# Filler products moved inside two triangular inverses, and a constant 512-column product added at eight places of one of them

## The reference, cut to what matters

```python
def second_block(x, ...):
    for layer in range(DEPTH):
        h = rms_norm_2(x, norm_g[layer])
        cols = split_columns(h @ w_in[layer])
        y_gdn = gdn_branch(cols, ...)      # unit lower triangular solve per chunk
        y_mla = mla_branch(cols, ...)      # softmax(q k^T) v
        y_rwkv = rwkv7_branch(cols, ...)   # a recurrence over the positions
        mix = concatenate([y_gdn, y_mla, y_rwkv]) * silu(cols['gate'])
        x = x + mix @ w_out[layer]
    return rms_norm_2(x, final_norm_g)
```

## Time and profile before

| | us |
|---|---|
| median of 3 runs | 1421.75 |
| lowest and highest | 1419.37 and 1426.42 |
| the profiled execution's own time | 1425.49 |
| its span | 1423.7 |
| TensorE (matmul) busy | 1324.1 (93% of the span) |
| VectorE busy | 745.7 (52%) |
| ScalarE busy | 344.9 (24%) |
| GpSimd busy | 51.5 (4%) |
| mean granted TensorE clock | 0.926 |

### The profile page before, as it was taken

One profiled execution on the slowest core, in us unless ns is written; L12 is line 12 of the kernel. 1 busy time (PEld: TensorE's weight loads), 2 busy tenths in 40 slices (PEclk: granted clock), 3 DMA queues, 4 the chain that ended last, 5 costly groups with the idle time before them and its releaser, 6 DMA issues. The chain is left out here.

```text
span 1423.7 us, 17706 instructions
## 1 busy us (share of the span) xinstructions
PE 1324.1 (93%) x6933; PEld 972.4 (68%) x6933; DVE 745.7 (52%) x1425; ACT 344.9 (24%) x745; POOL 51.5 (4%) x92
## 2 busy tenths in 40 slices
PE   4999989999989999999997998997999898997997
PEld 4877549994447765999443775685885775684783
DVE  0244366675350234677545388557544388557563
ACT  1233311210020242112002221343321221343222
POOL 2000000000000000000000001003000001002000
PEclk9989899999999999999999899998569999999579
DMA  8713106444453330545444331300011431300000
GB/s 254 243 55 118 60 2 219 158 159 176 175 177 118 119 118 1 194 163 177 177 177 162 105 117 60 119 1 1 0 46 57 155 115 59 119 2 1 1 1 30
DMA packets 65978, 149.21 MB, mean 105 GB/s; under 512 B 2225, under 2 KB 8263, under 8 KB 65895
## 3 DMA queue, kind: packets, MB, share of 16 engines
q1 hardware_dynamic: 62608, 141.67, 28.5%
q0 software_dynamic: 1216, 3.52, 1.0%
q10 hardware_dynamic: 2071, 2.87, 0.8%
HBM read 146.96 MB, written 1.07 MB: 104 GB/s over the span
## 5 line engine op out<-in xcount | busy, mean ns | idle before, releaser
L1305 ACT ACTIVATE region<-banks 128x384 f32<-128x384 f32 (+8 forms) x154 | 74.3, 482 | 363.9 <-PE banks L424 138.8
L424 PE MATMUL banks<-hnT,weight_slabs 128*128 128x256 f32 x672 | 154.9, 393 | 4.8 <-DVE hnT L1777 2.8
L424 PEld LDWEIGHTS banks<-hnT,weight_slabs 128*128 128x128 f32 x672 | 132.0, 198 | 27.3 <-issue 4.6
L474 PE MATMUL banks<-weight_slabs,region 128*128 128x512 f32 x256 | 115.1, 592 | 0.0
L1917 DVE TENSOR_TENSOR region<-banks,region 128x128 f32<-128x128 f32 x40 | 11.7, 292 | 152.8 <-PE banks L587 152.2
L474 PEld LDWEIGHTS banks<-weight_slabs,region 128*128 128x128 f32 x256 | 48.5, 190 | 60.3 <-issue 60.3
L474 PE MATMUL banks<-region 128*128 128x512 f32 x192 | 87.6, 592 | 0.0
L1760 DVE TENSOR_TENSOR region<-region 128x256 f32<-128x256 f32 (+23 forms) x160 | 75.5, 472 | 17.5 <-ACT region L1647 12.1
L1760 DVE TENSOR_TENSOR region<-weight_slabs 128x1024 f32<-128x1024 f32 x32 | 39.2, 1225 | 80.6 <-PE banks L474 76.4
L1760 DVE TENSOR_TENSOR region<-weight_slabs,region 128x1024 f32<-128x1024 f32 x64 | 78.2, 1222 | 1.1
L1261 POOL TENSOR_TENSOR region<-region,consts 128x240 f32<-128x240 f32 (+24 forms) x60 | 34.1, 588 | 1034.8 <-DVEq L1769 1000.9
(11 more groups left out here) (351 smaller groups left out, 2153.9 us busy)
## 6 DMA issues: line engine op xcount, KB each, us to landing
weight_slabs<-in_mlp_w SPq DMA_DIRECT2D x32, 2048.0 KB, 8.7
weight_slabs<-in_w_in SPq DMA_DIRECT2D x10, 2048.0 KB, 7.6
weight_slabs<-in_od_w_in SPq DMA_DIRECT2D x6, 2048.0 KB, 7.9
weight_slabs<-in_ev_w_in SPq DMA_DIRECT2D x5, 2048.0 KB, 8.0
weight_slabs<-in_w_out SPq DMA_DIRECT2D x4, 2048.0 KB, 8.1
weight_slabs<-in_ev_w_out SPq DMA_DIRECT2D x2, 2048.0 KB, 8.4
weight_slabs<-in_od_w_out SPq DMA_DIRECT2D x2, 2048.0 KB, 7.7
weight_slabs<-in_w_in SPq DMA_DIRECT2D x2, 2016.0 KB, 7.7
```

What stands on the lines that cost most here:

```text
L424: ins = mm(view(ps, b + i * S, (1, S)), view(slabs, o + k * width + c0, (1, P)), view(hnT, k * S, (1, S)), start=k == 0, stop=k == KC - 1)
L474: ins = mm(view(ps, b, (1, 512)), view(R, act + k * st, (1, P)), view(w, wt + k * step_, (1, 512)), start=n == 0 and k == 0, stop=n == 7 a ...
L1305: say(A(dst, view(ps, b, *(dims or ((1, n),)), np_=np_), ACT.Copy, scale=scale), read("scalar", *key))
```

## The change

In the RWKV inverse, `invert` calls `between("base", -1)` ahead of step 0, where `fill_inverse` now takes three steps of `dense`; the others of the base move to steps 4, 8, 10, 12 and 14 (eight in all as before, so far one at each even step). At the place ("Y", 1) there were two more steps of `dense`, for which nothing was left; two gate products come there now, and the four later places of the gate thus lose the last two of their eight products.

In the delta rule's inverse the gate products of the base steps 8 to 11 move: three to step 14, one to ("Yhalf", 0). A new helper `warm` issues one product of the identity with 512 constant columns into the bank that the ring "five" will hand out next, without taking it; its result is never read, as the next product of that bank starts it anew. It waits for the bank's last reader, as `open_` will. It is called once at eight places: ahead of step 0, after step 14, and at ("Z", 0), ("Y", 1), ("Z", 1), ("VT", 2), ("Z", 2) and ("X", 2). I call it the constant product.

```diff
@@ -402,6 +402,14 @@
             mm = nc.tensor.matmul
+
+            def warm(n, ring="short"):
+
+                b = RINGS[ring][turn[ring] % len(RINGS[ring])]
+                if b in held:
+                    pe.wait_ge(*at(reader.get(held[b], "bank_read_by_vector"), *held[b]))
+                for _ in range(n):
+                    mm(view(ps, b * 512, (1, 512)), IDENT, view(cst, 0, (1, 512)), start=True, stop=True)
@@ -768,6 +776,7 @@
                 H, NS = W.H, W.NS
+                between("base", -1)
                 for k in range(15):
@@ -970,12 +979,12 @@
                 def fill_inverse(what, n):
                     if what == "base":
-                        fill(1 - n % 2)
+                        fill({-1: 3, 4: 1, 8: 1, 10: 1, 12: 1, 14: 1}.get(n, 0))
                         if n == 7:
...
-                    elif (what, n) in (("Y", 0), ("Z", 0), ("Y", 1)):
+                    elif (what, n) in (("Y", 0), ("Z", 0)):
                         fill(2)
@@ -1121,10 +1130,11 @@
-                GATES = {("base", 8): 1, ("base", 9): 1, ("base", 10): 1, ("base", 11): 1, ("Yhalf", 0): 1, ("Zhalf", 0): 1, ("Yhalf", 1): 1, ("Zhalf", 1): 1}
+                GATES = {("base", 14): 3, ("Yhalf", 0): 2, ("Zhalf", 0): 1, ("Yhalf", 1): 1, ("Zhalf", 1): 1}
+                WARM = (("base", -1), ("base", 14), ("Z", 0), ("Y", 1), ("Z", 1), ("VT", 2), ("Z", 2), ("X", 2))
                 def mla_between(what, n):
-                    if what == "base":
+                    if what == "base" and n >= 0:
                         next(up_steps, None)
@@ -1134,6 +1144,8 @@
                         mla_transpose(PROBS[what, n])
+                    if (what, n) in WARM:
+                        warm(1, "five")
                     for _ in range(GATES.get((what, n), 0)):
```

## The result

The changed kernel takes 1373.96 us (median of 4 runs, 1372.09 to 1376.5), the kernel before 1421.89 (4 runs beside them, 1419.37 to 1426.42). The ratio is 0.9661, with a 95% interval of 0.9632 to 0.969: 48 us faster. The forecast was 1375, with a range from 1360 to 1406.

The account below looks back on a forecast made before the run. TensorE, busy almost without a break and often at half clock, was taken to set the length. The six parts sum to -49.7: 1375.8 against the profiled execution, 1372 against the median; forecast 1375, range 1360 to 1406.

Parts of the forecast that it names:

- Parts 1 and 2: RWKV inverse, both layers: moved products fill pauses and restore full clock; -9.7 for its base, -6.8 for its levels.
- The charge of 1.2 us for steps without fill: RWKV inverse's base: time added back because products left without fill wait for GpSimd's rows, 0.76 us each.
- the RWKV fills change nothing: Rival: GpSimd's picks set the RWKV base, so the RWKV gains halve; 1383 us, chance 0.10.
- Part 3: Delta rule inverse's base: four gate products leave steps 8 to 11, and the pause behind step 14 is filled; -5.8.
- Part 4: Level 0 of the delta rule's inverse: clock still falls at the longer pause ahead of Z; 20 us, net 0.
- only pauses matter: Rival: filled pauses alone keep the clock, also in level 0 (15.5 us) and the tail; 1361, chance 0.10.
- Part 5: Delta rule's inverse, level 1 to its end: full clock from dense products grouped ahead of Y; 22.4 us, -15.6.
- Part 6: Behind the inverse to the output products (tail): two thirds of the possible clock gain, -11.8, between 0 and -17.2.
- the clock stays low: Rival: narrow products keep the delta rule's inverse and tail at the low clock; 1415, against the median 1411, chance 0.14.
- slower: Rival: constant products all lengthen the path if the clock falls early and does not return; 1442, chance 0.04.

Follow-up runs that it names:

- without Z of level 0: The changed kernel without the constant product ahead of Z of level 0; 1381.31 us, ratio 0.9682.
- that pause: gates: The changed kernel with two gate products, moved from between the halves of Y and Z, replacing the constant product in level 0's pause; 1365.27 us, ratio 0.9564.
- the last two of the table: The kernel with gate products in level 0's pause, constant products kept only at three places (1379.27 us), or at all but the base's two (1375.33 us).

## Why the prediction was right

The cause it named holds: TensorE sets the length of these stretches, and the gain is the clock. Point by point:

- *Parts 1 and 2* (-9.7 and -6.8 forecast, -9.0 and -6.7 measured) hold: the RWKV edit alone won 15.7 us in its own stretches. The fall is gone in all 22 layers that have the edit. The edit filled the pause and regrouped the steps behind it at once, so that the pause alone was the cause, as I had taken it, fits but is not isolated. The charge of 1.2 us for steps without fill was the right kind: the row at 885.13 waits 0.83 us, though for VectorE's subtraction and not for GpSimd's picks, as the forecast had it. The rival "the RWKV fills change nothing" falls.
- *Part 3* (-5.8, measured -4.5; its own terms, -3.44 and +0.45 per layer, give -6.0) took the clock of the base as given. The base has a pause of its own, 2.84 us ahead of L1084, in which VectorE does six instructions of the attention (L2519 to L2525, 968.65 to 971.38) between two steps, and the clock fell behind it in both layers (0.93 for the base). Layer 3 had been free of that, so it won only 1.4. What stands behind B 14 put Y off by 0.37 us, where 0.45 had been said.
- *Part 4* (0 forecast, 20 us per level 0; measured 19.1, -2.0 in sum) had the mechanism right, against the rival "only pauses matter". The pause grew to 2.77 us (said 2.6), the constant product stood behind it and could not fill it, and the clock fell there. The work in that pause, put into free banks, then won 7 to 9 us, and the rival's figure for a level 0 at full clock (15.5) is near the 15.0 measured. Its time of 1361 was not reached, but another list came within 4 us of it (1365.27).
- *Part 5* (-15.6, measured -16.8) is right in size, and in that partly lucky, since in the changed kernel the reason given was not what acted. That reason was the dense group of scores, transposes and constant product ahead of Y of level 1. In both layers of the changed kernel the clock was back before that group (1003.6, the group starts at 1004.33), and four narrow products at each place kept it as well as wide ones. In four other layers the return does lie in that group's constant product: layer 2 of "without Z of level 0", "that pause: gates" and the last two of the table. But the group does not always do it: in layer 3 of four versions level 1 began at 0.50 in spite of it and took 27.4 to 32.3 us.
- *Part 6* was the mis-sized term: two thirds of the gain, -11.8, where all of it came, -16.1. The two thirds had no measurement behind them. The reasoning was right, that the engine reaches the last pauses at the upper level and falls there. What I had weighed against it, the products of 64 columns in the tail, is no danger once the pauses ahead are filled with wide products: 13.9 us in 16 of 16 cases, even behind a level 1 at 0.61.
- The rivals "the clock stays low" (1411) and "slower" (1442) are excluded: level 1 and tail are at 1.00. The version without constants shows those stretches at the low clock (31.2 and 21.9 us).

The sum erred by 1.7 us at the level of spans (-49.7 against -51.4), because parts 4 to 6 gave 7.5 more than was said, parts 1 to 3 gave 2.1 less, and the stages between and the untouched layers took 3.7. That 1375 came within 1.1 us of the measured time is thus in part luck: the mechanism was right, the largest error (-16.1 where -11.8 had been said) met smaller ones of the other sign, and the changed kernel's level 0 could have come out 2.6 us longer per layer with the same list.

## What to carry to other kernels

Read the granted clock per stretch before counting work: a stretch in which TensorE is busy without a break may still run at half speed, and then a product that computes nothing can pay for itself many times (sixteen of them, some 0.9 us each, gave 31.8 us). Put such work into the pause and not behind it: choose a bank whose reader is done, and take useful work for it where there is some; that was worth 7 to 9 us more. And when the clock decides, look at every layer and try a version that must not differ, since here the same list gave 19.1 or 21.7 us; an effect below some 10 us is not to be credited to an edit from one pair of kernels. The 7 to 9 us stand on more than that: level 0 took 13.4 to 17.5 us in all eight layers of the four kernels with its pause filled, and 18.0 to 21.7 in the other twenty.

## What the runs showed of the hardware that I had not expected

- The places where the clock came back are few. In level 0 and level 1 of all 28 layers it came back 31 times. 21 of these returns lie inside a product of 512 columns (a gate or a constant product) or at most 1.0 us behind one. The other ten lie in the block of products of 64 columns on 64 rows near the end of level 1 (L817 and L826, in the kernel before L808 and L817), which is where the 30 us at 0.50 ended. Neither is sure to do it: in the kernel before four gate products (998.3 to 1033.5) ran in that same stretch at 0.50 without a return.
- Four narrow products in a pause kept the clock in level 1 (1.00) and lost it ahead of the tail (0.66, in both layers). What differs, the pauses' place, or the products around them, wasn't tried; and the other version with narrow products there kept it at 1.00 in one layer and lost it in the other (0.61).
- A pause of 1.15 us ahead of Z left level 0 at 1.00 in one layer and at 0.79 in the other.
- The same list, at nearly the same time of the program (Z of level 0 at 996.8 and at 997.6), had its clock back at 1009.8 in one kernel and at 1003.6 in the other. The fall came 0.07 us later in the first, measured from Y (in layer 3 0.17 later); whether so little decides it the traces don't show, and no run here shifted a list in time and changed nothing else.
